# Feed-forward up loops: the low parts of the weight units and of the gated units are formed on VectorE instead of GpSimd

## The reference

```python
def conv_glu_ffn(a, w_up, conv_w, conv_b, w_down):
    u = a @ w_up                                   # 1024 -> 2 * 2816
    u = causal_depthwise_conv(u, conv_w, width 3) + conv_b
    gate, val = jnp.split(u, 2, axis=-1)
    return (jax.nn.silu(gate) * val) @ w_down      # 2816 -> 1024
```

## Time and profile before

| | us |
|---|---|
| median of three runs | 3087.27 (3078.12 to 3089.73) |
| the profiled execution | 3086.31 |
| span of its instructions | 3084.5 |
| mean granted PE clock | 0.964 of full speed |
| PE matmul busy | 2896.5 |
| DVE busy | 2047.5 |
| POOL busy | 1319.1 |
| ACT busy | 884.7 |

### The profile page before, as it was taken

The page is one execution under the profiler, slowest core; times in us unless marked ns, Lnnn a source line. Parts: engine busy times, 40 slices in busy tenths (PEclk is TensorE's granted clock), DMA queues, the critical chain, the costliest instruction groups (busy, mean ns, idle before and its releaser), DMA issues. The chain is left out here.

```text
span 3084.5 us, 58923 instructions
## 1 busy us (share of the span) xinstructions
PE 2896.5 (94%) x23024; PEld 2724.0 (88%) x23024; DVE 2047.5 (66%) x2708; ACT 884.7 (29%) x1333; POOL 1319.1 (43%) x598
## 2 busy tenths in 40 slices
PE   7899999999899979999877999999999999999999
PEld 6666899999888879999867999999989889799987
DVE  6777378861577747888979578882324535788840
ACT  3232222222333322222146322223212122322221
POOL 3111245564322224665453346565434243356563
PEclk9787899999999989999988999999999999999999
DMA  4011122233211112323220223323322222122232
GB/s 138 28 35 33 49 76 83 87 103 102 74 57 55 54 45 75 87 88 89 83 78 2 63 76 89 88 83 115 114 84 82 77 90 69 49 76 88 88 109 82
DMA packets 66413, 234.54 MB, mean 76 GB/s; under 512 B 8144, under 2 KB 8912, under 8 KB 65776
## 3 DMA queue, kind: packets, MB, share of 16 engines
q1 hardware_dynamic: 63648, 225.70, 24.6%
q10 hardware_dynamic: 2640, 7.02, 0.7%
HBM read 230.60 MB, written 2.10 MB: 75 GB/s over the span
## 5 line engine op out<-in xcount | busy, mean ns | idle before, releaser
L235 PE MATMUL ps<-xs,wr 128*128 128x264 f32 x13056 | 1641.4, 287 | 43.5 <-POOL wr L213 30.8
L213 POOL TENSOR_TENSOR wr<-raw,wr 128x1024 fp32r<-128x1024 f32 x422 | 1104.7, 2622 | 1339.1 <-ACT wr L205 1338.6
L235 PEld LDWEIGHTS ps<-xs,wr 128*128 128x128 f32 x13056 | 1606.0, 190 | 73.7 <-issue 45.0
L235 PE MATMUL ps<-hid,wr 128*128 128x264 f32 x5472 | 674.4, 285 | 20.1 <-POOL wr L213 12.0
L235 PEld LDWEIGHTS ps<-hid,wr 128*128 128x128 f32 x5472 | 669.5, 190 | 23.8 <-POOL wr L213 13.9
L205 ACT ACTIVATE wr<-raw 128x1024 fp32r<-128x1024 f32 x422 | 440.4, 1048 | 422.5 <-PE ps L235 349.1
L462 DVE SCALAR_TENSOR_TENSOR scr<-ub,convp,scr 128x528 f32<-128x528 f32 x176 | 442.8, 2516 | 24.0 <-DVE scr L459 0.6
L459 DVE SCALAR_TENSOR_TENSOR scr<-ub,convp,scr 128x528 f32<-128x528 f32 x176 | 216.8, 1232 | 26.6 <-DVE scr L456 17.4
L538 POOL TENSOR_TENSOR hid<-scr,hid 128x528 f32 x88 | 134.8, 1532 | 222.5 <-ACT hid L503 222.5
L500 ACT ACTIVATE scr<-scr 128x528 f32<-128x528 f32 x88 | 56.9, 646 | 416.3 <-DVE scr L462 416.3
L503 ACT ACTIVATE hid<-scr 128x528 f32 x88 | 56.8, 646 | 404.6 <-DVE scr L468 404.6
(11 more groups left out here) (268 smaller groups left out, 2323.8 us busy)
## 6 DMA issues: line engine op xcount, KB each, us to landing
raw<-in_stream SPq DMA_DIRECT2D x422, 512.0 KB, 3.6
work<-in_ret_tab ACTq DMA_DIRECT2D x4, 1056.0 KB, 5.7
h<-in_h SPq DMA_DIRECT2D x8, 264.0 KB, 6.2
out<-h SPq DMA_DIRECT2D x8, 256.0 KB, 4.5
work<-in_s_b ACTq DMA_DIRECT2D x1, 512.0 KB, 3.4
work<-in_s_c ACTq DMA_DIRECT2D x1, 512.0 KB, 4.6
convp<-in_convp ACTq DMA_DIRECT2D x4, 88.0 KB, 2.4
work<-in_mla_tab ACTq DMA_DIRECT2D x1, 264.0 KB, 2.5
```

What stands on the lines that cost most here:

```text
L213: pool.tensor_tensor(wr[:, s, 1].rearrange("p a b -> p (a b)"), raw[:, s, :], wr[:, s, 0].rearrange("p a b -> p (a b)").bitcast(F32), ALU. ...
L235: mm = pe.matmul(out[:, q], wr[:, slot, w, b0 + k], x[k][v][:, q * HALF:(q + 1) * HALF], start=start and k == 0 and p == 0, stop=stop and ...
```

## The change

In the up loops `split_unit` is called by DVE, ahead of the wait for the unit that it then takes out of PSUM. The low part of a hidden tile is formed by DVE too, in `low`, at the start of the other half (`low(0, i)` ahead of the split of q = 2, `low(1, i)` at the end of the pass). POOL has nothing in the up loops; it waits until the splits of DVE are done, and goes on with the units of the down part. The semaphore `up_pool` is gone, and its waits stand on `up_dve`. The orders of ACT, PE and SyncE are as before.

```diff
@@ ffn_pe
-            pe.wait_ge(up_pool.sem, up_pool.done(("lo", 1), end - 1))
-            late = {KT - 2 + j: (up_pool.sem, up_pool.done(("lo", j), end)) for j in range(2)}
+            pe.wait_ge(up_dve.sem, up_dve.done(("lo", 1), end - 1))
+            late = {KT - 2 + j: (up_dve.sem, up_dve.done(("lo", j), end)) for j in range(2)}
@@ ffn_dve
+            def low(j, i):
+
+                dve.wait_ge(up_act.sem, up_act.done(("hi", j), R + i))
+                lo = hid[:, bass.ds(i * 2 + j, 1), 1].rearrange("p a b -> p (a b)")
+                hi = hid[:, bass.ds(i * 2 + j, 1), 0].rearrange("p a b -> p (a b)")
+                dve.tensor_tensor(lo, scr[:, 3], hi.bitcast(F32), ALU.subtract).then_inc(up_dve.sem, up_dve.one(("lo", j)))
+
+            dve.wait_ge(lo_ready, u0 + AHEAD)
             with dve.Fori(0, KT // 2) as i:
                 for j in range(2):
                     for s in range(2):
                         q = 2 * j + s
+                        if q == 2:
+                            low(0, i)
+                        split_unit(dve, u0 + AHEAD + q, i, 4)
...
-                    dve.wait_ge(up_pool.sem, up_pool.done(("lo", j), R + i) - 1)
                     dve.tensor_tensor(scr[:, 3], scr[:, 2], scr[:, 1], ALU.mult)\
                        .then_inc(up_dve.sem, up_dve.one(("hidden", j)))
+                low(1, i)
...
-            dve.wait_ge(up_pool.sem, up_pool.done(("lo", 1), R + KT // 2 - 1))
+            dve.wait_ge(up_dve.sem, up_dve.done(("lo", 1), R + KT // 2 - 1))
@@ ffn_pool
-            R = layer * (KT // 2)
-            with pool.Fori(0, KT // 2) as i:
-                for s in range(4):
-                    split_unit(pool, u0 + AHEAD + s, i, 4)
-                    j = s // 2
-                    if s % 2 == 1:
-                        pool.wait_ge(up_act.sem, up_act.done(("hi", j), R + i))
-                        lo = hid[:, bass.ds(i * 2 + j, 1), 1].rearrange("p a b -> p (a b)")
-                        hi = hid[:, bass.ds(i * 2 + j, 1), 0].rearrange("p a b -> p (a b)")
-                        pool.tensor_tensor(lo, scr[:, 3], hi.bitcast(F32), ALU.subtract)\
-                            .then_inc(up_pool.sem, up_pool.one(("lo", j)))
             ug = u0 + 2 * KT
+            pool.wait_ge(lo_ready, ug + AHEAD)
```

More of the change, by code:

```diff
@@ L173, in trunk @@
         tail_low = Order(sem("tail_low"), ["lo"])
-        up_dve = Order(sem("up_dve"), [n for j in range(2) for n in
-                                       [(n, j, s) for s in range(2) for n in ("tap0", "tap1", "conv")] + [("hidden", j)]])
+        up_dve = Order(sem("up_dve"), [(n, 0, s) for s in range(2) for n in ("tap0", "tap1", "conv")] + [("hidden", 0), ("lo", 0)] +
+                       [(n, 1, s) for s in range(2) for n in ("tap0", "tap1", "conv")] + [("hidden", 1), ("lo", 1)])
         up_act = Order(sem("up_act"), [(n, j) for j in range(2) for n in ("silu", "hi")])
-        up_pool = Order(sem("up_pool"), [("lo", j) for j in range(2)], start=1)
         pads = sem("pads")
@@ L2357, in _ @@
         def _(pool):
-            pool.sem_inc(up_pool.sem, 1)
             for u in range(3):
```

## The result

| | us |
|---|---|
| kernel after, median of four runs | 3188.12 (3180.13 to 3194.34) |
| kernel before beside it, median of four | 3088.5 (3078.12 to 3090.62) |
| ratio, with its 95% interval | 1.0331 (1.0301 to 1.036) |
| profiled execution, before and after | 3086.31 and 3190.18 |

The kernel is 3.3% slower. The profiled executions differ by 103.9 us; forecast were 111.

What follows compares the result with a forecast made beforehand. It took DVE to pace the up loops. In-order waits for ACT make a half 13.40 us against 12.11; 3 x 28.4 + 26.2 = 111.4 us on 3086.3 gives 3198, bounds 3180 to 3233, widened to 3165 to 3235.

Steps and rivals of the forecast that it cites:

- The taps shorten to 0.77 us: Up loops, DVE: without POOL's subtractions beside it, the tap L462 takes 0.77 us instead of 2.68.
- A split of 1.22 us: Up loops: each weight-unit split on DVE takes 1.22 us, between 1.20 and 1.26.
- The waits: Up loops: DVE idles some 3 us a half waiting for ACT, some 1.7 us of it ahead of the odd split.
- A half of 13.40 us: Up loops: half a pass takes 13.40 us against 12.11, +1.29; bounds 13.2 to 13.8.
- The ends: Each layer's loop: first split behind the norm adds 1.15 us; PE's down part starts after 3.5 us, not 4.0, so -0.5.
- What lies around the loops: Down parts and mixers unchanged; DVE's preparation of the next mixer starts 1 to 2 us later, at most a few us in all.
- PE's pace of 11.7 us a half: Up loops: PE's own pace is 11.7 us a half, 12.11 less what it waits.
- rival (a): Up loops: DVE's new waits don't cost and the half falls to PE's 11.7 us; 37 us saved, 3050; chance 0.06.
- DVE is what turns this cycle: Up loops before the change: DVE paces the cycle of POOL's split, ACT's rounding, silu and conv that holds PE.
- Rival (d): Up loops: PE's clock falls as PE idles more; a half is 24 us, time 4150 if throughout; chance 0.03.

Runs made afterwards that it cites:

- third: Kernel before with only the weight units' splits moved to DVE, the hidden tile's low part staying on POOL: 3239.28 us, ratio 1.0497.
- tenth: Kernel after plus useless POOL subtractions in the up loops, four of 256 columns a unit on unshared data: 3234.14 us, ratio 1.0495.
- (1): Kernel after, but ACT rounds both units of a half before it waits for the silu: 3030.75 us, ratio 0.983.
- (2): Kernel after, but DVE splits the odd unit only after multiplying out the hidden tile: 3024.26 us, ratio 0.9808.
- fifth experiment: Kernel before, all low parts on POOL, but ACT rounds both units of a half before the silu: 3041.29 us, ratio 0.9881.

## Why the prediction was right, and where not

- **The taps shorten to 0.77 us.** Right: 769 ns both. That POOL's subtractions lengthen them is shown by the third and tenth experiments and not only by their lying side by side. The rule of the Trainium skill, "SBUF — State Buffer", section "Who interferes with whom", is borne out in both directions for operations that read two tiles: the later one waits (a split on DVE to 1.68 us, all but 0.15 us of its 1.23 behind the end of POOL's; an operation on POOL to 1.57 us).
- **A split of 1.22 us.** Right: all 176 took 1.226 us in the mean, on the line between the two widths of rows 6.
- **The waits.** Right: "some 1.7 us" ahead of the odd split was 1.66, and that they are the loss was shown by removing one (1) and filling it (2). The durations alone would have missed it: by work DVE had 10.3 us for a half of 12.1.
- **A half of 13.40 us.** It was 13.25 to 13.26 in layers 1 to 3 and 13.16 in layer 0. The term that was mis-sized is register work between conv and L468: I took the 0.21 us gap of rows 4, and it was 0.12 (1306.78 + 0.77, then 1307.67), as the wait on POOL's low part is no longer in between. The rest is hops, such as the one from a rounding's end to the split, 0.03 us and not 0.09. From the first L464 to the last L514's end the four loops grew by 94.7 us, where my sum has 3 x 27.7 + 25.5 = 108.6: 14 us too much.
- **The ends.** The first L464 comes 1.14 us after the split began in front of it (1.15 said), and PE's next unit starts 3.50 us after the last L514's end (3.5 said).
- **What lies around the loops.** My sum has 1.15 - 0.5 us a layer for it, 2.6 in all, and "a few us" on top. It grew by 9.2: 1.9 ahead of the loop of layer 0, 2.4 to 2.8 between two loops, -0.5 behind the last. So the sum has 6.6 us too little here, which hides half of the 14 us above: that the total came as near as 111 against 103.9 is in part luck. One step was the wrong way round: DVE's preparation of the next mixer starts 1.3 to 2.1 us behind the last L514's end, where it started 2.3 to 3.3 us behind the last L503's, so earlier and not 1 to 2 us later. What makes the stretches longer isn't shown. A candidate is PE's clock: its mean is 0.961 in the profiled execution and was 0.964 before. The 28 runs of the kernel before beside the experiments go from 3094.42 us at 0.960 to 3071.09 at 0.969, on average some 2 us for each 0.001 (an estimate from those runs).
- **PE's pace of 11.7 us a half.** Wrong, though it didn't enter the forecast: it is 11.58 (experiment 2). I took off 0.4 us, between the 0.29 that the matmuls wait and the 0.5 by the weight loads; the row of the weight loads was the better one, 12.11 - 0.49 = 11.62. With 11.58 the price of rival (a) is 11 us lower, 3039 and not 3050; the ratios of the first two experiments, in which DVE no longer waits behind the silu, give 3035 and 3028. The row of the weight loads, in the stretch of rows 4:

```profile
1292.34 11.63 PEld L235 LDWEIGHTS ps<-xs,wr 128*128 128x128 f32 x96 [0.49 <-issue]
```

- **"DVE is what turns this cycle", with the tap's length given.** Half right. DVE did hold the kernel before, but the fifth experiment shows that the tap's length itself hung on ACT's order, and rival (a)'s condition, the rounding no longer behind the silu, would have helped the kernel before as well.
- **The clock** stayed at 1.00 in all four loops with waits of 0.3 and 1.03 us ahead of PE's units. Rival (d) had no ground here. A stretch inside the loop of layer 1, columns as in rows 2:

```profile
1210.00:1480.00 270.00, 249.51 (x1986) 241.77 (x1985) 189.73 (x246) 63.94 (x81) 0.00 (x0) 1.00 0.27 80
```

## What to carry to other kernels

When work moves from an engine whose own waits cost next to nothing to one that paces the rest, price its waits and not only its durations: each wait stops the whole queue behind it. Here 176 splits of 1.2 us would have fitted, and one wait of 1.66 us a half turned a gain of 1.7% into a loss of 3.3%; placing the split where its input had long been ready gave 1.9%. And before moving work between engines, try the order of the engine that feeds both: rounding earlier on ACT gave 1.2% with nothing moved.

## What the runs showed of the hardware that I had not expected

That the blocking between POOL and DVE falls on either of them by who comes first, so that its price depends on the phase: the same work on POOL cost DVE 4.37 us of taps a unit in one order and 4.03 us in another, and POOL's own 0.61 us operation stretched to 1.57 us. A loop whose order of events repeats can lock into the bad phase for all its passes: in layer 1 of the kernel before every half from the second on takes 12.11 to 12.14 us. And the first tap, which reads one tile only, is held as well, 1.84 us against 0.56.
